# Column sums of the modulation vectors by accumulating transfers, for eight groups more

## The reference

```
x = x + jnp.square(jax.nn.relu(h @ w_up[l])) @ w_down[l]     # first block, MLP, d_ff = 8192
...
sh_m, sc_m, gt_m, sh_f, sc_f, gt_f = split(silu(c) @ w_mod + b_mod, 6)
csh_m, csc_m, ...                  = split(silu(c_ctx) @ w_mod + b_mod, 6)
h_lat = modulate(rms_norm_2(x, norm_mix_g), sh_m, sc_m)
h_ctx = modulate(rms_norm_2(y, norm_mix_g), csh_m, csc_m)
```

## Time and profile before

| | |
|---|---|
| median of 3 runs | 2602.07 us (2601.8 to 2602.39) |
| the profiled execution | 2600.4 us |
| its span in the trace | 2598.6 us |
| PE busy | 2576.3 us, 99% |
| DVE busy | 1838.8 us, 71% |
| transfers of the software queue (POOL) | 20.47 MB of 582.98 MB |

### The profile page before, as it was taken

The page is one execution under the profiler, slowest core; times in us unless marked ns, Lnnn a source line. Parts: engine busy times, 40 slices in busy tenths (PEclk is TensorE's granted clock), DMA queues, the critical chain, the costliest instruction groups (busy, mean ns, idle before and its releaser), DMA issues.

```text
span 2598.6 us, 35433 instructions
## 1 busy us (share of the span) xinstructions
PE 2576.3 (99%) x13200; PEld 2173.1 (84%) x13200; DVE 1838.8 (71%) x3327; ACT 1361.8 (52%) x2613; POOL 176.9 (7%) x233
## 2 busy tenths in 40 slices
PE   8999999999999999999999999999999999999999
PEld 7999889888888888888888898888788888888887
DVE  5677665777799999676867775677866665555555
ACT  5445575655545445455766566565544444444443
POOL 1011100021100000000011100000001111000000
PEclk9999999999999999999999999999999999999999
DMA  9796665688888888866777755544577777565564
GB/s 304 236 296 184 209 202 171 188 287 278 290 284 270 277 285 271 308 191 219 237 242 236 247 175 153 156 131 153 162 233 257 255 253 224 186 195 188 188 193 161
DMA packets 315707, 582.98 MB, mean 224 GB/s; under 512 B 30176, under 2 KB 38384, under 8 KB 315408
## 3 DMA queue, kind: packets, MB, share of 16 engines
q1 hardware_dynamic: 296768, 559.94, 66.0%
q0 software_dynamic: 18480, 20.47, 3.6%
q10 hardware_dynamic: 288, 0.31, 0.0%
HBM read 574.35 MB, written 2.10 MB: 222 GB/s over the span
## 4 chain that ended last, share of the span: by engine, by line
PE 96%; DVE 1%; ACT 1%; SPq 0%; DMA 0%; issue 0%; DVEq 0%; ACTq 0%
PE ps L1838 27%; PE ps L1840 26%; PE ps L1839 26%; PE ps L1827 3%; PE ps L1828 3%; PE ps L1829 3%; PE ps L1784 2%; PE ps L1920 1%; PE ps L1890 1%; PE ps L1909 1%; DMA raw<-in_w_in 0%; DVE wlo L2495 0%; PE ps L2035 0%; ACT whi L2157 0%; PE ps L2052 0%
## 5 line engine op out<-in xcount | busy, mean ns | idle before, releaser
L2495 DVE TENSOR_TENSOR wlo<-raw,whi 128x512 fp32r<-128x512 f32 x1712 | 1098.2, 686 | 536.5 <-ACT whi L2157 534.0
L2157 ACT ACTIVATE whi<-raw 128x512 fp32r<-128x512 f32 x1712 | 982.0, 624 | 817.1 <-PE ps L1840 527.1
L1838 PE MATMUL ps<-whi,th 128*128 128x512 f32 (+1 forms) x3124 | 1230.9, 394 | 2.2 <-ACT hA L2351 1.0
L1840 PE MATMUL ps<-whi,tl 128*128 128x512 f32 (+1 forms) x3124 | 1211.2, 388 | 0.0
L1839 PE MATMUL ps<-wlo,th 128*128 128x512 f32 (+1 forms) x3124 | 1210.3, 387 | 0.0
L1838 PEld LDWEIGHTS ps<-whi,th 128*128 128x128 f32 x3124 | 586.9, 188 | 122.2 <-issue 5.1
L1840 PEld LDWEIGHTS ps<-whi,tl 128*128 128x128 f32 x3124 | 586.5, 188 | 121.7
L1839 PEld LDWEIGHTS ps<-wlo,th 128*128 128x128 f32 x3124 | 587.4, 188 | 115.7 <-issue 1.0
L2513 DVE SCALAR_TENSOR_TENSOR acc<-raw,silc,acc 128x512 f32<-128x512 f32 x480 | 343.9, 746 | 10.5 <-DMA raw<-in_w_mod 6.0
L1827 PE MATMUL ps<-th,whi 128*128 128x256 f32 x640 | 186.0, 291 | 11.0 <-DVE wlo L2495 8.1
L1828 PE MATMUL ps<-th,wlo 128*128 128x256 f32 x640 | 181.6, 284 | 0.0
(11 more groups left out here) (320 smaller groups left out, 1296.7 us busy)
## 6 DMA issues: line engine op xcount, KB each, us to landing
raw<-in_w_in SPq DMA_DIRECT2D x231, 512.0 KB, 3.9
raw<-in_w_down SPq DMA_DIRECT2D x216, 512.0 KB, 4.6
raw<-in_w_mod SPq DMA_DIRECT2D x192, 512.0 KB, 4.5
raw<-in_w_gate_up SPq DMA_DIRECT2D x176, 512.0 KB, 3.5
raw<-in_w_up SPq DMA_DIRECT2D x128, 512.0 KB, 4.6
raw<-in_w_out SPq DMA_DIRECT2D x64, 512.0 KB, 3.8
raw<-in_xattn_wkv SPq DMA_DIRECT2D x16, 512.0 KB, 3.4
raw<-in_w_in SPq DMA_DIRECT2D x16, 268.0 KB, 4.1
```

The costliest lines, as they stand in the source:

```text
L1838: pe.matmul(p, xh, wh[:, c, c0:n], start=a and (form != "both" or tb == 0), stop=False, skip_group_check=True)
L1840: ins = pe.matmul(p, xl, wh[:, c, c0:n], start=False, stop=z, skip_group_check=True)
L2157: self.e.activation(t.his[g % NHI][:, n * c:n * c + n], t.raws[j % NRAW][:, n * c:n * c + n], ACT.Copy).then_inc(*s.hi.up((g, c)))
L2495: self.e.tensor_tensor(t.los[j % NRAW][:, at], t.raws[j % NRAW][:, at], t.his[g % NHI][:, at].bitcast(F), ALU.subtract).then_inc(*s.lo.up( ...
```

## The change

- Groups 0 to 7 are summed like the others, by folds and scatters on POOL. `mod_total` and `mod_turn` are gone on PE, ACT and DVE.
- The accumulators lie in pairs, `acc01` and `acc23`. An even group 0 to 7 uses both halves of `acc01`, an odd one both of `acc23`. Groups 8 to 23 use one half of `acc01`, as before.
- One fold transfer takes both halves of a pair (rows of 4 KB and not 2 KB).
- The scatters of a pair, four to `mod` and four to `modx`, are issued in a row; `modx` now starts with the bias in it.
- The rate during the MLP is 0.42 and not 0.5.

```
-        self.acc = [sb(f"acc{i}", (r_a if i < 2 else r_s + 8192) + 2048 * i, [512]) for i in range(4)]
+        self.accs = [sb("acc01", r_a, [2, 512]), sb("acc23", r_s + 12288, [2, 512])]
+        self.acc = [self.accs[i // 2][:, i % 2, :] for i in range(4)]
...
     def mod_step(self):
         j, kc = self.todo.pop(0)
-        vs = [j % 2, 2 + j % 2] if j < 8 else [j % 2]
+        vs = [2 * (j % 2), 2 * (j % 2) + 1] if j < 8 else [j % 2]
...
     def mod_sum(self, j, vs):
         for _ in range(LOOK):
             yield
-        if len(vs) == 1:
...
-        while not self.side_quiet():
+        rows = 64
+        while rows:
+            self.mod_fold(j, vs, rows)
             yield
-        bank = self.side().take()
-        self.mod_total(j, vs, bank)
...
-        self.mod_turn(j, vs, bank)
-        bank.give((self.s.mcol, j), *([(self.s.mcolx, j)] if len(vs) > 1 else []))
+            rows //= 2
+        self.mod_scatter(j, vs)
         for v in vs:
-            self.acc_after[v], self.acc_late[v] = [(self.s.mtt, j)], False
+            self.acc_after[v], self.acc_late[v] = [(self.s.mcolf if v == vs[0] else self.s.mcolx, j)], False
...
-        self.rate = 0.5
+        self.rate = 0.42
         self.todo = self.todo + [(j, kc) for j in range(8) for kc in range(8)]
...
+        pair, n = t.accs[vs[0] // 2], len(vs)
+        a = slice(0, 2) if n > 1 else slice(vs[0] % 2, vs[0] % 2 + 1)
+        po.dma_start(pair[0:rows, a, :], pair[rows:2 * rows, a, :], accum_op=ALU.add).then_inc(*s.fold.up((j, rows), 16))
...
+        if len(vs) > 1 and j:
+            self.wait_ge(*s.mcolx.at(j - 1))
+        for dst, v, made in ((t.mod, vs[0], s.mcolf), (t.modx, vs[-1], s.mcolx))[:len(vs)]:
+            for a in range(4):
+                po.dma_start(dst[:, 4 * j + a:4 * j + a + 1], t.acc[v][0:1, 128 * a:128 * a + 128], accum_op=ALU.add).then_inc(
+                    *made.up(j if a == 3 else (j, a), 16))
```

More of the change, by code:

```diff
@@ L95, in __init__ @@
             new("hi_made"), new("lo_made"), new("chunk_multiplied"), new("first_rows_multiplied"), new("mod_added"))
-        self.msum, self.mrow, self.mtt, self.mcol, self.mcolx = (
-            new("mod_summed"), new("mod_row"), new("mod_turned"), new("mod_column"), new("mod_column_ctx"))
-        self.fold, self.mcolf = new("mod_folded"), new("mod_scattered")
+        self.fold, self.mcolf, self.mcolx = new("mod_folded"), new("mod_scattered"), new("mod_scattered_ctx")
         self.ld_id, self.ld_gain, self.ld_rest, self.ld_c, self.ld_late = (
@@ L289, in __init__ @@
             small("hT", [2, 32]), small("kcT", [32]), small("ssp", [2, 4]), small("st", [16]), small("sm", [96]))
[L290 to L291 removed]
+        self.dec, self.sink, self.ln4, self.sm2 = (
+            small("dec", [4, 12]), small("sink", [8]), small("ln4", [8]), small("sm2", [8]))
         self.hK, self.hJ = sb("hK", z, [2, 512]), sb("hJ", r_s + 11264, [2, 128])
@@ L356 @@
     start_loads = load_mem_part = load_mem_rows = silu_columns = spread_rstd = mem_square = heads_direct = finish = load_xt_part = load_x_rows = late_loads = load_ctx = load_final = load_masks = load_bounds = load_qkg = skip
-    issue = halves_in = scale_in = split = mod_add = mod_total = mod_turn = mod_fold = mod_scatter = multiply = turn_scale = turn_piece = raw_piece = settle_scale = settle_halves = turn_low = stat = root = reduce_sums = skip
+    issue = halves_in = scale_in = split = mod_add = mod_fold = mod_scatter = multiply = turn_scale = turn_piece = raw_piece = settle_scale = settle_halves = turn_low = stat = root = reduce_sums = skip
     idle_products = heads_silu = roots_next = rows_out = residual_add = spatial_weights = skip
@@ L534, in mod_cols @@
     def mod_cols(self, j0, j1):
-        return [(self.s.mcol if j < 8 else self.s.mcolf, j) for j in range(j0, j1)]
+        return [(self.s.mcolf, j) for j in range(j0, j1)]
     def mods_until(self, j1):
@@ L1696, in start_loads @@
         po.dma_start(t.cols2[:, :], a["columns"][:, 96:165]).then_inc(*s.ld_rest.up("cols2", 16))
-        po.dma_start(t.mod[:, 32:96], a["columns"][:, 197:261]).then_inc(*s.ld_rest.up("mod", 16))
-        po.dma_start(t.bmc[:, :], a["columns"][:, 165:261]).then_inc(*s.ld_rest.up("all", 16))
+        po.dma_start(t.mod[:, :], a["columns"][:, 165:261]).then_inc(*s.ld_rest.up("mod", 16))
+        po.dma_start(t.modx[:, :], a["columns"][:, 165:197]).then_inc(*s.ld_rest.up("all", 16))
     def late_loads(self):
@@ L1754, in load_qkg, with mod_fold, mod_scatter @@
         po.dma_start(t.qkg[:, 1, :], a["k_norm_g_2"].broadcast_to([128, 128])).then_inc(*s.ld_qkg.up(name, 16))
-    def mod_fold(self, j, v, rows):
+    def mod_fold(self, j, vs, rows):
         t, s, po = self.t, self.s, self.e
         if rows == 64:
-            self.wait_all([self.mod_end(j, 7, [v])])
+            self.wait_all([self.mod_end(j, 7, vs)])
         else:
             self.wait_ge(*s.fold.at((j, 2 * rows)))
-        po.dma_start(t.acc[v][0:rows, :], t.acc[v][rows:2 * rows, :], accum_op=ALU.add).then_inc(*s.fold.up((j, rows), 16))
-    def mod_scatter(self, j, v):
+        pair, n = t.accs[vs[0] // 2], len(vs)
+        a = slice(0, 2) if n > 1 else slice(vs[0] % 2, vs[0] % 2 + 1)
+        po.dma_start(pair[0:rows, a, :], pair[rows:2 * rows, a, :], accum_op=ALU.add).then_inc(*s.fold.up((j, rows), 16))
+    def mod_scatter(self, j, vs):
         t, s, po = self.t, self.s, self.e
@@ L1847, in idle_products @@
             self.e.matmul(bank.tile[:, :], t.ident[:, :], t.mskt[:, 0:512], start=True, stop=True, skip_group_check=True)
[L1849 to L1866, removed]
     def turn_piece(self, name, j, xp, here, bank, op, g, sh, gtok):
```

32 lines of the change are left out of this document (1 added, 31 removed).

## The result

The changed kernel takes **2675.78 us** (median of 4 runs, 2674.66 to 2677.04); the kernel before, run beside it, 2602.22 us (2601.8 to 2602.39). The ratio is 1.0287, 95% interval [1.0275, 1.0299]: slower by 73.6 us. The forecast was 2668, range 2640 to 2704.

What follows compares the result with a forecast made beforehand. PE was taken to bound the kernel, busy for 2576.3 of 2598.6 us. Terms -8.8 + 19 + 53 + 2.6 = +65.8 gave 2666 us on the profiled execution, 2668 on the median; range 2640 to 2704.

Steps and rivals of the forecast that it cites:

- PE's saving: Column sums and transposes of eight groups leave PE, 1.10 us each: 8.8 us less.
- first wait: Group 0 waits for group 15's scatters in `acc01`; PE dry for 19 us, bounds 9 to 34.
- second wait: Context gain waits for group 7's chain before the fourth `down`; PE dry for 53 us, bounds 37 to 82.
- restarts: PE starts slowly after each of two stops, 1.3 us each: 2.6 us in all.
- Groups 1 to 6: nothing: Chains of these groups end before their pair's next use, 58 us after the last addition: no cost.
- the 1.5 us for pairs: Extra for a pair's wider rows over a whole chain of seven folds: 1.5 us, between nothing and 4.
- Folds at the loaded price all along: Every fold in both waits takes 4.7 us a step whatever the load: 2699 us; chance 0.12.
- All at the light price: Every transfer in both waits at its light price, the lower bounds: 2642 us; chance 0.07.
- Only the end bites: DVE runs further ahead at 0.42, so the wait at group 0 shrinks below 5 us: 2652 us; chance 0.05.
- Faster after all: Both chains end inside DVE's lead, leaving only the 8.8 us taken from PE: 2593 us; chance 0.03.

Runs made afterwards that it cites:

- experiment 1: Changed kernel with the two accumulator pairs swapped, so that group 0 takes `acc23`: 2655.44 us, ratio 1.0207.
- experiment 6: Kernel before, with every column sum and each transpose made twice on PE: 2606.26 us, ratio 1.0019.
- Experiments 2 and 3: Changed kernel with the rate back at 0.5: 2621.03 us; the same with the accumulator pairs also swapped: 2597.53 us.
- the last experiment: Ninth run: changed kernel with pairs swapped, MLP rate 0.48, and groups 8 to 15 begun at 0.56 instead of 0.5: 2593.01 us, ratio 0.9969.
- experiment 4: Kernel before with the rate 0.42 alone, groups 0 to 7 still summed on PE: 2621.3 us, ratio 1.0076.

## Why the prediction was right

The sum was +65.8, on the profiled execution; the delay of the matmuls came to +75.7. By its terms:

| term | predicted | measured |
|---|---|---|
| PE's saving | -8.8 | -8.73 (experiment 1) |
| first wait | 19 | 18.80 |
| second wait | 53 | 61.72 |
| restarts | 2.6 | 2.8 + 1.1 |

**PE's saving** was read from distances between starts. The busy time would have given a price several times as high; experiment 6 refutes it from the other side. But 1.10 is the price of the first copy, changeover included, and not a price per matmul.

**The first wait** came out step by step. T is 730.8. PE was dry at T + 14.4 (14.8 predicted); the chain made four loaded steps and three light ones and ended at T + 30.8 (31); PE started at T + 33.2 (33.7). Experiment 1 removed this wait and nothing else.

**Groups 1 to 6: nothing** held at 0.42. Experiments 2 and 3 show the same chains at 0.5, where they do bite.

**The second wait** had the right mechanism, and every part that the prediction named was there: seven leftover chunks, group 6's chain first, then group 7's, then the gain, then the first split. It was 8.7 us too short. With 0 at the end of PE's work (1142.2):

| | predicted | measured |
|---|---|---|
| group 6, last addition | -16 | -15.7 |
| group 7, last addition | +10 | +15.3 |
| group 6, folds done | +18 | +22.2 |
| group 7, folds done | +43.5 | +51.1 |
| gain of the context | +51.6 | +59.6 |
| PE starts | +53.5 | +61.7 |

The term that was mis-sized is the price of a fold, in two places: 4.2 us are lost by the end of group 6's folds, 3.4 more by the end of group 7's, 0.6 behind them.

Group 6's chain took 37.6 us from its first fold and not 34.4: its first step alone 10.1, right behind two loads of the context (1121.25 and 1121.99), the next two 6.2 and 6.7. The prediction had dismissed these loads as an issue of 0.7 us each; that is what they cost POOL, and not, it seems, what they cost the fold queued behind them.

Group 7's folds took 24.0 us, where the prediction had 2.4 for each and 1.5 in all for the wider rows of a pair, 18.3. The first took 6.5, of which 2.3 are the end of the issue of group 6's scatters (the prediction had counted these separately, so 21.7 stand against its 18.3); then 3.4, 3.1, 3.1, 2.9, 2.6 and 2.4. Load is not the reason: the chunks were in by then, as the prediction had it, and nothing but this chain moved. The steps get shorter with the size of the fold, from 128 KB for the second to 4 KB for the last, and the kernel of experiment 1 shows the same seven within 0.02 us. The 2.4 had been read from a small fold: the earlier trace rows is the sixth of a group with rows of 2 KB, 4 KB in all, and the three light steps of the first stop belong to folds of 8, 4 and 2 KB. So the 1.5 us for pairs, for which the prediction had no row, is what was too small. Whether the width of the rows or the bytes of the fold set the price, the runs do not separate.

The late last addition of group 7 (DVE got to the chunks at -3.3 and not at -8.5) did not matter, since POOL took the group only at 1169.2, +27.

**The restarts** cost 2.8 and 1.1 us. The rows are matmuls with 256 columns, which lose 0.09 us each at the start; those after the stops have 512, and come 0.43 us apart and not 0.227: 0.2 us more for each of some 14, and of 7 the second time. That the second came out near the 1.3 of the prediction is luck: the loss of each was twice as large, and half as many were slow.

**The rivals.** Folds at the loaded price all along (2699) is refuted by the steps of 2.3 to 2.4 in the first stop. All at the light price (2642) is refuted by the same rows and by group 6. The page of the Trainium skill on which it leaned, "DMA: Bandwidth & Descriptors", section "Anatomy of one DMA — SWDGE (gpsimd) path", would give a pair's seven folds about 15 us as an estimate; group 7's took 24.0 us (1169.23 to 1193.27) with no other transfer beside them, so the measurement decides against it. "Only the end bites" (2652) is not what happened, but it is almost exactly the kernel of experiment 1 (2655.4). "Faster after all" needed both chains inside the cover; in the last experiment neither of these two chains holds anything up (a lag of 3 us elsewhere is left), and it comes to 2593.01 beside 2600.93 of before, the time that the rival named.

What decided the sign was the order of work. Folding on POOL alone does bring PE's saving; the first stop comes from the choice of accumulators, and the second from the rate, of which 0.42 leaves seven chunks over. About 19 us of the second were lost to the leftover chunks, and the kernel before loses about as much, 20.4, to the same rate (experiment 4); the other 44 are the new chains.

## What to carry to other kernels

Work moved off a full engine to a slow chain is free only if the chain ends before its first reader in the order that is written, so count for the last group, and for the first that reuses a buffer, how far the reader stands behind, and add what that chain does once: loads queued ahead of it and the group before it on the same queue. A lower rate of side work thins out a queue, but it must still finish the work: compare chunks left with ticks left times rate before choosing it, and leave room for one whole chain. Find the cover of a wait by walking the waiting engine's list and the bound engine's list together, since a small instruction behind the wait (here the spread of two statistics) can end it at one chunk.

## What the runs showed of the hardware

- Accumulating transfers within SBUF, each waiting for the one before, from issue to issue: with nothing else moving, 3.4 us for 128 KB, 3.1 for 64 and for 32, 2.9 for 16, 2.6 for 8 and 2.4 for 4 KB (group 7, rows of 4 KB), and 2.4, 2.4 and 2.3 for 8, 4 and 2 KB (group 15, rows of 2 KB). While chunks are loaded (share 0.89) group 15's larger folds took 4.3 to 5.3, and at a share of about 1 the second and third of group 6 took 6.2 and 6.7.
- The first fold of a pair, 256 KB, took 7.8 to 12.4 us in nine cases in which two context loads of 512 KB were issued on the same queue in the 6 us ahead of it, and 11.8, 16.2 and 16.4 behind four such loads (experiments 9, 2 and 3). Without them, with chunks being loaded, it took 4.8 to 9.9. The ranges overlap, and that these loads are the cause was not tried by moving them away.
- After a stop of 18.8 us, and after one of 61.7, PE's clock is granted at 0.50 and the same matmuls start 0.43 us apart instead of 0.227. That is the 1.2 GHz level and not the 2.4 GHz one. The longer stop did not cost more: 7 slow matmuls against about 14. The Trainium skill, page "TensorE: Matmul & The Clock Gate", section "Part 1: The HAM clock gate (the "warmup" mystery)", gives 426.7 ns from start to start for 512 columns on the throttled array; the trace agrees.
- Sixteen narrow matmul entries (128 x 128, 32 columns of weights) take 0.43 to 0.58 us, though the trace gives each 0.27 us of busy time. Changing from wide matmuls to them and back costs about 0.26 us more, once.
